# A trunk with product-key experts: heads combined in groups, and the diagonal matmuls as four 64x64 blocks

## The reference, cut to what matters

```python
def peer_block(x, w_q, q_g, sub_keys, u_tab, v_tab):
    q = rms_norm((x @ w_q).reshape(t, 8, 256), q_g).reshape(t, 8, 2, 128)
    s = jnp.einsum('thcd,hcnd->thcn', q, sub_keys)
    s_top, i_top = lax.top_k(s, 16)
    cand = (s_top[:, :, 0, :, None] + s_top[:, :, 1, None, :]).reshape(t, 8, 256)
    cand_idx = (i_top[:, :, 0, :, None] * 128 + i_top[:, :, 1, None, :]).reshape(t, 8, 256)
    best, pos = lax.top_k(cand, 16)
    idx = jnp.take_along_axis(cand_idx, pos, axis=-1)
    g = jax.nn.softmax(best, axis=-1)
    act = gelu(einsum('thkd,td->thk', u_tab[idx], x))
    return einsum('thk,thkd->td', g * act, v_tab[idx])
x = layer_norm(ALPHA * x1 + peer_block(x1, ...), ln2_g, ln2_b)
```

## Time and profile before

| | us |
|---|---|
| median of 3 runs | 3860.18 (3859.78 to 3864.34) |
| the profiled execution | 3858.03 |
| its span, first to last instruction | 3856.2 |
| PE busy | 3131.0 (81%) |
| VectorE busy | 2357.5 (61%) |
| ScalarE busy | 1455.2 (38%) |
| GpSimd busy | 1179.2 (31%) |
| moved by DMA | 1307.45 MB, of them 1140.92 MB by the gathers |
| mean granted TensorE clock | 0.953 |

### The profile page before, as it was taken

How to read it: one execution, slowest core, us unless ns; L and a number is a source line. 1 busy time by engine, 2 the same in 40 slices (tenths; PEclk the granted TensorE clock), 3 DMA queues, 4 the chain that set the end, 5 groups by cost and what they waited for, 6 DMA issues and landing times.

```text
span 3856.2 us, 33162 instructions
## 1 busy us (share of the span) xinstructions
PE 3131.0 (81%) x9276; PEld 1531.6 (40%) x9276; DVE 2357.5 (61%) x5270; ACT 1455.2 (38%) x4235; POOL 1179.2 (31%) x1099
## 2 busy tenths in 40 slices
PE   7999447987888788879878887898789878889876
PEld 4678323442343334334433443344234423333321
DVE  8501475676568566855785578557756762336854
ACT  1111124334434443444344434443444343333433
POOL 0000024333333333434343333343333321113332
PEclk9999779998999899999998999999989999999999
DMA  5321459999999999999999999999899987779998
GB/s 139 85 80 49 145 231 415 378 416 364 404 391 412 359 375 420 378 399 372 419 371 391 374 417 357 408 374 417 357 391 379 416 348 271 271 269 382 410 378 348
DMA packets 239992, 1307.45 MB, mean 339 GB/s; under 512 B 41170, under 2 KB 69106, under 8 KB 90034
## 3 DMA queue, kind: packets, MB, share of 16 engines
q0 software_dynamic: 156672, 1140.92, 73.2%
q1 hardware_dynamic: 81442, 159.13, 11.9%
q10 hardware_dynamic: 1696, 5.27, 0.4%
HBM read 1285.65 MB, written 17.97 MB: 338 GB/s over the span
## 4 chain that ended last, share of the span: by engine, by line
DMA 34%; PE 25%; DVE 16%; ACT 9%; issue 4%; SPq 2%; POOL 1%; DVEq 0%; POOLq 0%; ACTq 0%
DMA UV<-in_peer_uv,icur 33%; PE psum L1024 16%; DVE junk L1348 7%; PE psum L951 3%; ACT D L1126 2%; PE psum L971 2%; PE psum L929 1%; ACT wge L1123 1%; ACT E L1034 1%; ACT L1121 1%; DMA wq<-in_cache_k 1%; DVE E L1309 1%; DVE E L1314 1%; SPq L800 1%; ACT ge L1121 1%
## 5 line engine op out<-in xcount | busy, mean ns | idle before, releaser
L1024 PE MATMUL psum<-UV,D 128*128 128x512 f32 (+1 forms) x4352 | 2118.2, 624 | 590.9 <-ACT D L1126 558.2
L860 POOL DMA_INDIRECT UV<-in_peer_uv,icur x1088 | 1173.6, 1079 | 2270.8 <-PE psum L1024 2036.8
L1348 DVE CUSTOM_DVE_ANT_0 junk<-UV,x 128x1024 bf16<-128x1024 f32 x1088 | 1333.5, 1226 | 868.6 <-DMA UV<-in_peer_uv,icur 797.3
L1024 PEld LDWEIGHTS psum<-UV,D 128*128 128x128 f32 (+1 forms) x4352 | 789.0, 194 | 1701.2 <-issue 1658.8
L1121 ACT ACTIVATE ge<-acts 128x1 f32<-128x1 f32 x1088 | 220.0, 202 | 1765.9 <-DVE acts L1348 1763.5
L1126 ACT ACTIVATE D<-ident,wge 128x128 f32<-128x128 f32 x1024 | 411.1, 401 | 33.4
L1123 ACT ACTIVATE wge<-ge,gcur 128x1 f32<-128x1 f32 x1088 | 320.5, 295 | 35.3
L971 PE MATMUL psum<-wq,aT 128*128 128x256 f32 (+1 forms) x1152 | 263.6, 382 | 1.2 <-ACT aT L1073 1.2
L971 PEld LDWEIGHTS psum<-wq,aT 128*128 128x128 f32 (+1 forms) x1152 | 212.9, 186 | 67.7 <-issue 33.4
L297 PE MATMUL psum<-xT,w_in_sb 128*128 128x384 f32 (+1 forms) x384 | 120.4, 477 | 14.1 <-DMA xT<-in_x_T 14.1
L308 PE MATMUL psum<-w_in_sb,xT 128*128 128x256 f32 (+1 forms) x576 | 129.6, 383 | 0.0
(11 more groups left out here) (296 smaller groups left out, 2261.3 us busy)
## 6 DMA issues: line engine op xcount, KB each, us to landing
wq<-in_peer_w_q SPq DMA_DIRECT2D x72, 1024.0 KB, 9.1
UV<-in_peer_uv,icur POOLq DMA_INDIRECT x1088, 10.3
wq<-in_cache_k SPq DMA_DIRECT2D x64, 256.0 KB, 6.7
vrows<-in_cache_v SPq DMA_DIRECT2D x64, 256.0 KB, 6.4
w_in_sb<-in_w_in SPq DMA_DIRECT2D x8, 1024.0 KB, 7.2
x<-in_x_all SPq DMA_DIRECT2D x9, 512.0 KB, 8.4
w_out_sb<-in_w_out SPq DMA_DIRECT2D x1, 4096.0 KB, 17.5
out<-x ACTq DMA_DIRECT2D x8, 512.0 KB, 6.9
```

What stands on the lines that cost most here:

```text
L860: pool.indirect_dma_start(out=UV[:, n % RING, :], out_offset=None, in_=table, in_offset=bass.IndirectOffsetOnAxis(ap=icur[:, t % 2, k:k + ...
L1024: ins = pe.matmul(bank[6 + e][:rows, :], D[:, n % RING, :rows], UV[:, n % RING, DM + 512 * e:DM + 512 * e + 512], start=k == 0, stop=k == ...
L1348: dve.tensor_tensor_reduce(out=junk[:, :], in0=UV[:, n % RING, 0:DM], in1=x1[:, t % 2, :], scale=1.0, scalar=0.0, op0=ALU.mult, op1=ALU.ad ...
```

## The change

**Groups.** Heads are combined in three groups: head 0, heads 1 and 2, and heads 3 to 7 of a prompt tile. The sample tile takes its heads in the order 0, 4, 1, 5, 2, 6, 3, 7 and groups the first two, the next two and the last four of them. A combine has 5 steps instead of 10, over the group's heads alone, and increments `cur_ready` once for each group; each gather waits for its own group's. Heads follow one another every 5 steps (4 in the sample tile).
**Placement.** Only the steps up to the end of the first group's combine (`lead`: 78 steps, 88 in the sample tile) run ahead of a tile's experts. The rest runs in the tile's own slots from k = 0. The next tile's front begins in slot 50 (40 for the sample tile), and its first `cur_ready` comes in slot 127. The sample tile's copies to partitions 64 to 127 are made for each group.
**Blocks.** `D` has 64 columns. PE multiplies four 64x64 diagonal blocks instead of one of 128x128: two row halves r, each with two column halves, into four quadrants of banks 6 and 7. `dve_sum` has four operations of 64 rows instead of two of 128, with a wait behind each; in the sample tile it adds both row halves.

```diff
-        D = sb("D", [P, RING, P])
+        D = sb("D", [P, RING, SR])
...
+        def order(t):
+
+            return range(EH) if t < NT else (0, 4, 1, 5, 2, 6, 3, 7)
+
+        def groups(t):
+
+            return ((0, 1), (1, 3), (3, 8)) if t < NT else ((0, 2), (2, 4), (4, 8))
+
+        def group_of(t, k):
+            p = k // TOP if t < NT else 2 * (k // TOP)
+            return next(g for g, (p0, p1) in enumerate(groups(t)) if p < p1)
...
+                if t == NT and e == EH - 2:
+                    sp_spread(sp, 0)
...
+            p0, p1 = groups(NT)[g]
+            wait(sp, "cur_ready", 3 * NT + g + 1)
+            for cur in (icur, gcur):
+                pairs = cur[:, NT % 2, TOP * p0:TOP * p1].rearrange("p (q s k) -> p s q k", s=2, k=TOP)
+                sp.dma_start(pairs[SR:P, 0, :, :], pairs[0:SR, 1, :, :]).then_inc(sem("spread"), 16)
...
-            if k == 0:
-                wait(pool, "cur_ready", t + 1)
-                if t == NT:
-                    wait(pool, "spread", 48)
+            g = group_of(t, k)
+            wait(pool, "cur_ready", 3 * t + g + 1)
+            if t == NT:
+                wait(pool, "spread", 16 + 32 * (g + 1))
...
             for e in range(2):
-                ins = pe.matmul(bank[6 + e][:rows, :], D[:, n % RING, :rows], UV[:, n % RING, DM + 512 * e:DM + 512 * e + 512],
-                                start=k == 0, stop=k == steps(t) - 1)
+                for r in range(2):
+                    q = 64 * (e ^ r)
+                    ins = pe.matmul(bank[6 + r][q:q + 64, :], D[64 * r:64 * r + 64, n % RING, :],
+                                    UV[64 * r:64 * r + 64, n % RING, DM + 512 * e:DM + 512 * e + 512],
+                                    start=k == 0, stop=k == steps(t) - 1)
             ins.then_inc(sem("vsum_done"), 1)
...
-            act.activation(D[:, j, :rows], ident[:, :] if rows == P else id2[:, :], ACT.Copy, scale=wge[:, j:j + 1])\
+            act.activation(D[:, j, :], id2[:, :], ACT.Copy, scale=wge[:, j:j + 1])\
...
             if r == 1:
-                wait(act, "qs_ready", t + 1)
-                act.activation(small[:rows, 40:48], small[:rows, 32:40], ACT.Sqrt).then_inc(sem("qr_ready"), 1)
+                wait(act, "qs_ready", 3 * t + g + 1)
+                act.activation(small[:rows, 40 + p0:40 + p1], small[:rows, 32 + p0:32 + p1], ACT.Sqrt).then_inc(sem("qr_ready"), 1)
...
             for c, (op, n) in enumerate(((ALU.logical_shift_right, 4), (ALU.bitwise_and, 15))):
-                if r == 3 + 3 * c:
...
+                if r == 2 * c:
...
-                if r == 4 + 3 * c:
...
+                if r == 2 * c + 1:
...
+            halves = ((0, 0), (1, 1)) if t < NT else ((0, 0), (0, 1))
             for e in range(2):
...
+                for d, r in halves:
+                    q = 64 * (e ^ r)
+                    out = x[64 * d:64 * d + 64, 512 * e:512 * e + 512]
+                    scale = ALPHA if t < NT or r == 0 else 1.0
+                    step(dve.scalar_tensor_tensor(out=out, in0=out, scalar=scale, in1=bank[6 + r][q:q + 64, :],
+                                                  op0=ALU.mult, op1=ALU.add))
...
+        def heads_from(t, e):
+            return base(t) + 15 + (5 if t < NT else 4) * e
...
+        def combine_at(t, g):
+            return heads_from(t, groups(t)[g][1] - 1) + 10
+
+        def lead(t):
+
+            return combine_at(t, 0) + 5
+
+        def fronts(t, k):
+
+            own = [(t, lead(t) + k)]
+            return own + [(t + 1, k - NK + lead(t + 1))] if t < NT and k >= NK - lead(t + 1) else own
...
-                for k in range(front_end(0)):
-                    dve_front(dve, step, 0, k)
+                for f in range(lead(0)):
+                    dve_front(dve, step, 0, f)
                 for t in range(NT + 1):
                     for k in range(steps(t)):
                         if t and k == 2:
                             dve_sum(dve, step, t - 1)
                         dve_expert(dve, t, k)
-                        if t < NT:
-                            dve_front(dve, step, t + 1, k)
+                        for u, f in fronts(t, k):
+                            dve_front(dve, step, u, f)
```

More of the change, by code:

```diff
@@ L790, in number, with column @@
             return NK * t + k
+        def order(t):
[5 more added lines that the diff above has]
+            return next(g for g, (p0, p1) in enumerate(groups(t)) if p < p1)
+        def column(t, k):
+            return k if t < NT else 2 * (k - k % TOP) + k % TOP
         def landed(n):
@@ L1016, in pe_expert @@
             n = number(t, k)
-            rows = rows_of(t)
             if k == 0:
@@ L1282, in dve_head, with dve_combine, wide @@
                 dve_topk(dve, step, cand[:rows, :], sc2[:rows, :], best[:rows, e, :], pos[:rows, e, :])
-        def dve_combine(dve, step, t, r):
+        def dve_combine(dve, step, t, g, r):
             rows = rows_of(t)
-            eq = Ef[:rows, 0:NK * TOP].rearrange("p (e k i) -> p e k i", e=EH, k=TOP)
+            p0, p1 = groups(t)[g]
+            ng = p1 - p0
+            cols = slice(TOP * p0, TOP * p1)
+            eq = Ef[:rows, 0:ng * TOP * TOP].rearrange("p (e k i) -> p e k i", e=ng, k=TOP)
+            scale = small[:rows, 40 + p0:40 + p1]
+            top = small[:rows, 48 + p0:48 + p1]
+            def wide(v):
+                return v.rearrange("p (e u) -> p e u", u=1).broadcast_to((rows, ng, TOP))
@@ L1288, in dve_combine @@
             if r == 0:
-                wait(dve, "q_copied", EH * t + EH)
-                dve.tensor_scalar(small[:rows, 32:40], small[:rows, 24:32], 1.0 / (2 * NKEY), EPS, ALU.mult, ALU.add)\
-                   .then_inc(sem("qs_ready"), 1)
-                step(dve.tensor_copy(itf[:rows, :, :], it[:rows, :, :]))
+                wait(dve, "q_copied", EH * t + p1)
+                dve.tensor_scalar(small[:rows, 32 + p0:32 + p1], small[:rows, 24 + p0:24 + p1], 1.0 / (2 * NKEY), EPS,
+                                  ALU.mult, ALU.add).then_inc(sem("qs_ready"), 1)
@@ L1301, in dve_combine @@
-                dve.tensor_tensor(best[:rows, :, :], best[:rows, :, :],
-                                  small[:rows, 40:48].rearrange("p (e u) -> p e u", u=1).broadcast_to((rows, EH, TOP)), ALU.mult)\
+                wait(dve, "qr_ready", 3 * t + g + 1)
+                step(dve.reciprocal(scale, scale))
+                step(dve.tensor_copy(top, best[:rows, p0:p1, 0]))
+                step(dve.tensor_tensor(best[:rows, p0:p1, :], best[:rows, p0:p1, :], wide(top), ALU.subtract))
+                dve.tensor_tensor(best[:rows, p0:p1, :], best[:rows, p0:p1, :], wide(scale), ALU.mult)\
@@ L1334, in dve_front @@
             else:
-                if k == 0:
+                if f == 0:
                     dve_sample_setup(dve, step)
-                dve_sample(dve, step, *divmod(k, ST))
-            dve_output(dve, step, t, k - base(t))
-            for e, r in heads_at(t, k):
+                dve_sample(dve, step, *divmod(f, ST))
+            dve_output(dve, step, t, f - base(t))
+            for e, r in heads_at(t, f):
                 dve_head(dve, step, t, e, r)
-            dve_combine(dve, step, t, k - combine_at(t))
+            for g in range(3):
+                dve_combine(dve, step, t, g, f - combine_at(t, g))
         def dve_expert(dve, t, k):
@@ L1376, in base, with heads_at @@
             return 4 * AT if t < NT else ST * DB + 6
[L1378 to L1390 removed]
+        def heads_from(t, e):
+            return base(t) + 15 + (5 if t < NT else 4) * e
+        def heads_at(t, f):
+            return [(e, f - heads_from(t, e)) for e in range(EH) if 0 <= f - heads_from(t, e) < 10]
+        def combine_at(t, g):
[5 more added lines that the diff above has]
+            return own + [(t + 1, k - NK + lead(t + 1))] if t < NT and k >= NK - lead(t + 1) else own
         with nc.Block() as block:
```

130 lines of the change are left out of this document (56 added, 74 removed).

## The result

| | before | changed |
|---|---|---|
| median, us | 3861.24 | 3908.99 (3902.06 to 3910.27) |
| ratio | | 1.0119, interval 1.0101 to 1.0136 |
| the profiled execution | 3858.03 | 3909.71 |
| its span | 3856.2 | 3907.1 |
| PE busy | 3131.0 | 2720.8 |

The account below looks back on a forecast made before the run. Expert gathers fill DMA most of the time, with losses in a few recurring places; -52.8 + 4.8 - 8.5 + 9 + 16.5 + 0.5 = -30.5 us gave 3830 us, range 3774 to 3895.

Parts of the forecast that it names:

- item 1: Prologue: only steps 73 to 77 precede the first gather, which starts at 484.5 instead of 537.4 us: -52.8 us.
- Items 2 and 3: Slots 122 to 127 with the gap: 29 us against 16.4; slots 0 to 9, VectorE-bound: 43.5 us against 30.3.
- Item 4: Slots 10 to 49: gathers and loads, less 8.5 us for gathers landed ahead, plus 2 for stutter: 103 us.
- Item 5: Slots 50 to 97, attention without layer norm 2: 123 us; slots 98 to 121: the old 73.8 less PE's gain.
- Item 6: Diagonal matmuls: an expert's eight records take 0.86 us, not 4 x 0.43; 1.7 us per tile saved at output projection.
- Item 7: Sum of a plain tile, 370.5 us: six take 2223 against 2231.5, -8.5 us; tile 0 +4.8 us.
- Item 8: Tile 7: 556 us, +9; its sample attention 311 instead of 327.4, 12 us of that from shorter experts.
- Item 9: Tile 8 and the tail: tile 8 takes 179.7 us against 163.2, +16.5; the tail +0.5.
- (a): Rival, more gain: VectorE's pile-up is partly absorbed, 8 us per tile over seven tiles: 3774 us; chance 0.17.
- (b): Rival, slower: ScalarE's table loads make VectorE wait for roots, 2.5 us each, 60 in all: 3890 us; chance 0.22.
- (c): Rival: the blocks' column halves don't overlap, so gains in tile 7 and the outputs go: 3856 us; chance 0.14.
- (d): Rival: the blocks run one by one, 3.4 us per expert on PE: over 4600 us; chance 0.02.

## Why the prediction was wrong

**What bounds the kernel, item 1.** Right: the first gather at 483.14 (484.5), the first dot 54.3 us earlier (52.8). **Items 2 and 3.** Right: 29.5 (29) and 43.7 (43.5). That VectorE becomes the bound there is shown by the ring: with five, six and seven slots k 0 to 9 takes 43.4, 43.7 and 43.4.

**Item 4 is the step that failed**: 111.4 for 103 in each plain tile (669.5 for 618 in six of them, where the kernel before has 669.3). It set 40 gathers, four loads and a credit for the ring against the whole stretch and let DMA run at 419 GB/s (one gather in 2.5 us) throughout. By bytes, the four stretches moved 43.5 MB (each length by its GB/s), which take 103.8 us at 419. The forecast had 36.5 gathers and four loads, 42.5 MB in 101 us, and 2 us for stutter. So 2.8 us are bytes that had not come ahead, and 7.6 us are rate: 2.5 in k 10 to 29, 1.5 in 30 to 34, 2.7 in 35 to 39 and 1.0 in 40 to 49. Less the 2 for stutter, that is the 8.4. Of the 7.6, 3.5 lie where the engines' share is 1.00: there the 419 GB/s was simply too much, as 409 in k 50 to 97 shows too. The other 4.1 lie where DMA has gaps.

The rate is the larger fault, and its gaps lie in the mean. VectorE's 71 us for 25 slots and DMA's 72 for them looked like a tie in which each covers the other. In fact they are bound in turn: DMA in k 10 to 29 (share 1.00), VectorE in 30 to 34 (18.5 us for five dots and the combine), dots back to back on what the ring holds in 35 to 39 while DMA falls to 280 GB/s, DMA again from 40 on. What one engine lacks in its stretch, the other's next stretch doesn't give back, beyond what the ring holds.

The bytes are the credit. I took 3.5 gathers, from a slot that returns "about 10 us" after its dot starts, "landing near 6". That landing belongs to an idle queue at a boundary (5.7 in the earlier trace rows). Where the ring should fill, a landing takes 8.5 to 10.9 us, so a slot is back after 13 to 16 us (PE's end 3.4 to 4.3 after the dot starts, the issue about 1), and six gathers at 2.5 us are 15. So two or three gathers had landed at dot 10, not 3.5. PE's wait for the sum takes its part: the change lengthened slots 0 to 2 ahead of it, which no row of before shows, but the 7.7 us of GpSimd were there to be read.

The term occurs in tile 0 (+9.2), in six plain tiles (+51.4) and in tile 7 (k 10 to 39: 87.1 for 79), 69 of the 81 us missed.

**Item 5.** Right: 123.0 and 72.3. **Item 6.** The rate was right, 1.09 with its tail for 0.86. Its worth was read at the wrong place: I looked for time on PE behind the output projection, 1.7 us per tile. In the changed placement with six slots the blocks give 5 to 10 us per plain tile, 6.7 in the mean and most of it in k 50 to 97, where item 6 said that slots wait for DMA and gain nothing; with seven slots they give none.

**Item 7** follows item 4: a plain tile 379.9 for 370.5, so six of them lose where 8.5 us of gain was forecast. **Item 8.** The sample attention took 320.0 us, not 311. This is the second step that failed: the 12 us from shorter experts didn't come, since PE's wait for key pages grew instead. In tile 7 of the changed kernel, and then of the same kernel with full diagonals:

```profile
PE psum L921 <- DMA wq<-in_cache_k: 48.1, 7, 9.3
...
PE psum L921 <- DMA wq<-in_cache_k: 21.6, 6, 4.4
```

against 23.0 in the earlier trace rows. With full diagonals the sample attention takes 319.1 us, with blocks 320.0. In all the runs this wait is 20 to 24 us with full diagonals and 48 to 59 with blocks, whatever the placement and the ring. I had put only four of six experts into its shadow; all six lie in it. **Item 9.** 182.3 for 179.7, small as it had the same credit but much VectorE-bound time that needs none.

**The rivals.** (a) had it that the pile-up is partly absorbed; it is the opposite, the ring absorbs less than I took. (b) named the right side with the wrong cause. The table loads did grow from 151 to 227, but VectorE's waits for roots didn't: layer norm 2's in tile 5, 4.64 before, and a combine's are now

```profile
2402.46 0.17 DVE L1237 RECIPROCAL small<-small 128x1 f32<-128x1 f32 x1
...
2413.43 0.17 DVE L1330 RECIPROCAL small<-small 128x2 f32<-128x2 f32 x1
```

both without idle time ahead of them. That gain of some 26 us in all (eight waits) lies inside k 0 to 9, where it was counted. (c) and (d) are refuted by the 1.09 us. What came true is the sentence that a mis-sized pile-up would make it wrong above all, eight times over.

**The clock.** It fell as feared: 0.50, the level of 1.2 GHz, in k 30 to 39, where PE does nothing but short experts. It costs TensorE time: the query matmuls, which the edit doesn't touch, are busy for 307.3 us with blocks and 264.9 with full diagonals. That it costs the kernel time is not shown, and not excluded. At that level an expert in blocks takes 1.98 us; in full form at the upper level it takes, in the run with full diagonals,

```profile
2439.98 1.95 PE L1044 MATMUL psum<-UV,D 128*128 128x512 f32 x4 [0.83 <-ACT D L1149]
...
2450.54 3.42 PE L1044 MATMUL psum<-UV,D 128*128 128x512 f32 x4 [3.04 <-ACT D L1149]
```

1.95, and 3.42 at the lower. So a block expert at the lower level is as fast as a full one at the upper. With seven slots the kernels at mean clocks of 0.793 and 0.946 need the same time, which leaves room for a gain of the blocks and a price of the clock that cancel.

**What stays open.** Seven slots ran only with layer norm 2 on the constants of layer norm 1; a kernel that finds room for all four was not tried. Nor was the sum ahead of slot 2, which would end GpSimd's 10.5 us. Why the blocks cost time in tile 7, and why they bring so little in the old order, is not known. No run holds the clock and changes the blocks, or the reverse.

## What to carry to other kernels

In a kernel bound by gathers, sum stretch by stretch with the larger of VectorE's and DMA's time, and never over a stretch in which the bound changes; what the ring can carry from one stretch to the next is read from issue to landing in that stretch, not at an idle queue. Set beside it what the same slots took before the change. The return of a slot doesn't tell by itself whether a slot is missing, because the queue is in it: in k 50 to 97 of the changed placement one dot takes 2.80, 2.56 and 2.52 us with five, six and seven slots (means of tiles 1 to 6), which makes 14.0, 15.4 and 17.6 us for a turn of the ring. Only the run with one slot more or less tells. Where the ring is short, one slot is worth more than most edits, and an edit that only makes a slot's user shorter is worth a lot or nothing, depending on the ring. Moved work then pays only if it is laid so flat that no few slots of it exceed the gathers beside them.

## What the runs showed of the hardware that was not expected

- The median from issue to landing of a 1 MB gather follows the number of gathers under way: 8.5, 10.3 and 12.6 us in the kernel before with rings of five, six and seven; 5.7 from issue to dot into an idle queue.
- Five gathers at a time are too few for the engines, and six are just about enough: the attention's slots of tile 5 ran at 375, 409 and 419 GB/s with five, six and seven (length 135.0, 123.0 and 121.4 us).
- DMA that is full is not always at its best rate: k 10 to 29, with the weight loads in it, show a share of 1.00 at 401 GB/s, k 50 to 97 without them 1.01 at 409. Whether the loads are the cause was not tried.
- Four 64x64 fp32 blocks run at once: 1.09 us for eight records at 2.4 GHz, 1.98 at 1.2 GHz, and TensorE's mean granted clock is 0.781 with them and 0.943 in the same kernel with full diagonals.
